# Index scores of a sparse-attention layer: every fourth weighted part summed by GpSimd instead of the vector engine

## What is computed

```python
logits = jnp.einsum('bqhd,bsd->bqhs', iqb, ik)
index = jnp.einsum('bqh,bqhs->bqs', iwb, jax.nn.relu(logits)) * idx_scale
index = jnp.where(causal[None], index.astype(jnp.float32), -jnp.inf)
_, sel = lax.top_k(index, topk)
```

## Time and profile before

| | |
|---|---|
| median of 3 runs | 3709.44 us (3705.83 to 3711.16) |
| profiled execution | 3711.52 us |
| its span, first to last instruction | 3709.0 us |
| mean granted TensorE clock | 0.968 of full speed |
| busy: PE, DVE, ACT, POOL | 3461.9, 2405.3, 1793.0, 1235.4 us |
| index units on VectorE, L1769 and L1772 | 38 and 266 |

### The profile page before, as it was taken

One profiled execution on the slowest core, in us unless ns is written; L12 is line 12 of the kernel. 1 busy time (PEld: TensorE's weight loads), 2 busy tenths in 40 slices (PEclk: granted clock), 3 DMA queues, 4 the chain that ended last, 5 costly groups with the idle time before them and its releaser, 6 DMA issues. The chain is left out here.

```text
span 3709.0 us, 55779 instructions
## 1 busy us (share of the span) xinstructions
PE 3461.9 (93%) x19082; PEld 2960.1 (80%) x19082; DVE 2405.3 (65%) x4983; ACT 1793.0 (48%) x3056; POOL 1235.4 (33%) x1944
## 2 busy tenths in 40 slices
PE   6999978899999999999999799699999999999998
PEld 6999867778888878788878688588888788888876
DVE  9999556667666766676774244765654657665354
ACT  3323235677776677767767333333333333333232
POOL 5454134454443432333222033433221425332021
PEclk9999899899999999999999899899999999999999
DMA  4344310000000000000000245332224452332444
GB/s 147 113 149 150 97 33 24 17 24 17 17 17 10 17 17 8 17 8 5 7 9 4 103 146 157 116 125 80 91 80 165 163 172 73 109 103 89 139 137 170
DMA packets 189699, 289.61 MB, mean 78 GB/s; under 512 B 33394, under 2 KB 129778, under 8 KB 189426
## 3 DMA queue, kind: packets, MB, share of 16 engines
q1 hardware_dynamic: 185300, 285.11, 23.4%
q10 hardware_dynamic: 4128, 1.05, 0.1%
HBM read 211.15 MB, written 74.97 MB: 77 GB/s over the span
## 5 line engine op out<-in xcount | busy, mean ns | idle before, releaser
L1669 ACT ACTIVATE shared<-a_ps_st 128x512 f32<-128x512 f32 x716 | 437.5, 615 | 288.4 <-PE a_ps_st L1555 147.7
L2712 PE MATMUL f_ps<-f_x_hi,f_w_hi 128*128 128x512 f32 x1232 | 482.5, 392 | 22.5 <-DVE f_w_lo L2849 22.5
L2712 PE MATMUL f_ps<-f_x_lo,f_w_hi 128*128 128x512 f32 x1232 | 481.6, 391 | 0.0
L2712 PE MATMUL f_ps<-f_x_hi,f_w_lo 128*128 128x512 f32 x1232 | 481.4, 391 | 0.0
L1579 PEld LDWEIGHTS a_ps_o<-a_vsl,shared 128*128 128x128 f32 x2176 | 294.5, 199 | 19.7 <-DVE a_fin L1886 0.7
L1377 POOL TENSOR_SCALAR a_tk<-a_tk,a_halves 128x1 f32<-128x1 f32 x336 | 106.1, 316 | 584.5 <-ACT a_junk_a L1676 582.7
L1579 PEld LDWEIGHTS a_ps_o<-a_dv,shared 128*128 128x128 f32 x2176 | 286.1, 194 | 12.5
L2712 PEld LDWEIGHTS f_ps<-f_x_hi,f_w_hi 128*128 128x128 f32 x1232 | 232.7, 189 | 73.0 <-DVE f_w_lo L2849 24.9
L1579 PE MATMUL a_ps_o<-a_vsl,shared 128*128 128x65 f32 x2176 | 286.1, 276 | 0.0
L1579 PE MATMUL a_ps_o<-a_dv,shared 128*128 128x65 f32 x2176 | 277.0, 271 | 0.0
L294 PE MATMUL p_ps<-pw_hi,px_hi 128*128 128x384 f32 (+1 forms) x672 | 228.1, 339 | 47.6 <-DVE pw_lo L399 30.4
(11 more groups left out here) (370 smaller groups left out, 8738.9 us busy)
## 6 DMA issues: line engine op xcount, KB each, us to landing
f_raw<-in_w_down SPq DMA_DIRECT2D x88, 512.0 KB, 3.5
px_raw<-in_x_t SPq DMA_DIRECT2D x48, 512.0 KB, 4.5
f_raw<-in_w_gate SPq DMA_DIRECT2D x44, 512.0 KB, 4.9
f_raw<-in_w_up SPq DMA_DIRECT2D x44, 512.0 KB, 4.8
g_scratch<-f_gs SPq DMA_DIRECT2D x22, 1024.0 KB, 7.6
f_raw<-g_scratch SPq DMA_DIRECT2D x88, 256.0 KB, 3.5
z_scratch<-p_z SPq DMA_DIRECT2D x16, 768.0 KB, 3.4
o_scratch<-a_oacc SPq DMA_DIRECT2D x32, 256.0 KB, 2.1
```

Source lines behind the costliest of these rows:

```text
L1669: act.activation(p_t[:, s % PT_RING, :], ps_st[s % ST_BANKS][:, :], ACT.Exp, scale=SCALE).then_inc(exp_done, 1)
L2712: mm = pe.matmul(out[:, :], w[:, j, k * P:(k + 1) * P], x[:, j, k], start=(k == 0 and i == 0), stop=(k == 3 and i == 2))
```

## The change

Of the index jobs, those whose number in `relu_no` leaves 3 when divided by 4 are summed by GpSimd, the others by VectorE as before. GpSimd has no single operation for it here: it multiplies the relu buffer by the weight in place (L1268), waits for its own semaphore, and adds the buffer to the index row (L1271). For h=0 it multiplies straight into the row (L1261). Instead of one semaphore that counts all sums there is one for each engine, and each wait looks up which engine's sum it means (`wait_sum`). GpSimd does the units of a step at the end of its own step s, after the threshold moves, the gathering and the splits of that step; VectorE still holds its units until the next step.

76 of the 304 jobs move: 32 of 512 columns, 16 of 384, 14 of 256 and 14 of 128. Where a tile has four chunks it is always the fourth chunk that GpSimd sums, for all eight heads.

```diff
--- before.py
+++ after.py
@@ -669,6 +669,7 @@
 NMAX_RING = 12
 PV_LAG = 3
 ONE_ROW = 94
+POOL_EVERY = 4
 SEL_COLS = 30
 SIDE_COST = {"max": 550, "cmax": 600, "idx": 680, "prep": 600, "aug": 150}
 CHORE_COST = {"peak": 0, "above": 300, "rank": 1150, "pick": 1250, "set": 900, "room": 0}
@@ -1064,6 +1065,12 @@
             reader.append(("evac", n_evac))
             if job[0] == "aug":
                 aug_no[job[1]] = turn_no[job]
+    sum_no, sums_by = {}, {"pool": 0, "dve": 0}
+    for job, r in relu_no.items():
+        who = "pool" if r % POOL_EVERY == POOL_EVERY - 1 else "dve"
+        sums_by[who] += 1
+        sum_no[job] = (who, sums_by[who])
+    nth_idx = list(relu_no)
     last_max = {job[1]: job for step in sides for job in step if job[0] == "max"}
     last_idx = {t: ("idx", t, IDX_HEADS - 1, plan.chunks[t] - 1) for t in range(2, TILES)}
     finish_at = {}
@@ -1177,7 +1184,7 @@
         exp_done = sem("a_exp_done")
         pv_done = sem("a_pv_done")
         relu_done = sem("a_relu_done")
-        index_done = sem("a_index_done")
+        index_done = {who: sem(f"a_index_{who}") for who in ("pool", "dve")}
         search_set = sem("a_search_set")
         counted = sem("a_counted")
         thr_moved = sem("a_thr_moved")
@@ -1227,6 +1234,41 @@
         def mask_d_value(t):
 
             return t + 1 if t < 2 else 2 + chunk_no[(t, plan.chunks[t] - 1)] + 1
+
+        def wait_sum(eng, job):
+
+            who, value = sum_no[job]
+            eng.wait_ge(index_done[who], value)
+
+        def wait_index(eng, t):
+
+            for c in range(plan.chunks[t]):
+                wait_sum(eng, ("idx", t, IDX_HEADS - 1, c))
+
+        def index_unit(eng, job):
+
+            _, t, h, c = job
+            who, _ = sum_no[job]
+            w = min(CHUNK, (t + 1) * P - c * CHUNK)
+            r = relu_no[job]
+            eng.wait_ge(relu_done, r + 1)
+            dst = index[t % 2][:, c * CHUNK:c * CHUNK + w]
+            weight = iw[:, t % 4, h:h + 1]
+            if h == 0:
+                eng.wait_ge(gate_in, 2 * (t + 1))
+                if t >= 4:
+                    eng.wait_ge(mask_d_done, mask_d_value(t - 2))
+                eng.tensor_scalar(dst, relu[:, r % RELU_RING, 0:w], weight, None, ALU.mult).then_inc(index_done[who], 1)
+            else:
+                wait_sum(eng, ("idx", t, h - 1, c))
+                part = relu[:, r % RELU_RING, 0:w]
+                if who == "dve":
+                    eng.scalar_tensor_tensor(dst, part, weight, dst, ALU.mult, ALU.add).then_inc(index_done[who], 1)
+                else:
+                    eng.tensor_scalar(part, part, weight, None, ALU.mult).then_inc(own, 1)
+                    begin.pool_owned[0] += 1
+                    eng.wait_ge(own, begin.pool_owned[0])
+                    eng.tensor_tensor(dst, dst, part, ALU.add).then_inc(index_done[who], 1)
 
         @block.sync
         def _(sp):
@@ -1344,7 +1386,7 @@
                 if t >= 4:
 
                     if t >= 6:
-                        pool.wait_ge(index_done, relu_no[last_idx[t - 4]] + 1)
+                        wait_index(pool, t - 4)
                     pool.wait_ge(fin_done, number[("S", t - 4, 1)] + 1)
                 at = KEY_COLS + IDX_DIM
                 pool.tensor_copy(iw[:, t % 4], zk[:, at:at + IDX_HEADS]).then_inc(gate_in, 1)
@@ -1441,6 +1483,9 @@
                         move_threshold(*c)
                     else:
                         waiting.append(c)
+                for job in sides[s]:
+                    if job[0] == "idx" and sum_no[job][0] == "pool":
+                        index_unit(pool, job)
 
         @block.tensor
         def _(pe):
@@ -1659,7 +1704,7 @@
                 act.wait_ge(side_done, scan_no[job] + 1)
                 if r >= RELU_RING:
 
-                    act.wait_ge(index_done, r - RELU_RING + 1)
+                    wait_sum(act, nth_idx[r - RELU_RING])
                 act.activation(relu[:, r % RELU_RING, 0:w], ps_side[side_no[job] % SIDE_BANKS][:, 0:w], ACT.Relu).then_inc(relu_done, 1)
 
             def exps(s):
@@ -1753,28 +1798,10 @@
                 settle()
                 dve.tensor_scalar(tile[:, 4 * g:4 * g + 4, col:col + 1], src, 1e20, None, ALU.min).then_inc(aug_set, 1)
 
-            def index_unit(job):
-                _, t, h, c = job
-                w = min(CHUNK, (t + 1) * P - c * CHUNK)
-                r = relu_no[job]
-                dve.wait_ge(relu_done, r + 1)
-                dst = index[t % 2][:, c * CHUNK:c * CHUNK + w]
-                weight = iw[:, t % 4, h:h + 1]
-                if h == 0 and c == 0:
-                    dve.wait_ge(gate_in, 2 * (t + 1))
-                if h == 0:
-                    if t >= 4 and c == 0:
-
-                        dve.wait_ge(mask_d_done, mask_d_value(t - 2))
-                    dve.tensor_scalar(dst, relu[:, r % RELU_RING, 0:w], weight, None, ALU.mult).then_inc(index_done, 1)
-                else:
-                    dve.wait_ge(index_done, relu_no[("idx", t, h - 1, c)] + 1)
-                    dve.scalar_tensor_tensor(dst, relu[:, r % RELU_RING, 0:w], weight, dst, ALU.mult, ALU.add).then_inc(index_done, 1)
-
             def peak(t, c):
 
                 if c == 0:
-                    dve.wait_ge(index_done, relu_no[last_idx[t]] + 1)
+                    wait_index(dve, t)
                 mine(dve.tensor_reduce(peaks[:, c:c + 1], index[t % 2][:, chunk_cols(t, c)], AX.X, ALU.max, apply_absolute_value=True))
 
             def set_search(t):
@@ -1899,16 +1926,16 @@
                 before = len(held)
                 for job in sides[s]:
                     if held and side_no[job] - side_no[held[0]] > SIDE_BANKS:
-                        index_unit(held.pop(0))
+                        index_unit(dve, held.pop(0))
                         before -= 1
                     if job[0] == "max":
                         mask(job)
                         if job == last_max[job[1]]:
                             set_aug(job[1])
-                    elif job[0] == "idx":
+                    elif job[0] == "idx" and sum_no[job][0] == "dve":
                         held.append(job)
                 while before > 0:
-                    index_unit(held.pop(0))
+                    index_unit(dve, held.pop(0))
                     before -= 1
                 for name, t, c in plan.chores[s]:
                     if name == "peak":
```

## The result

| | before | after |
|---|---|---|
| median of the runs (range) | 3710.3 us (3705.8 to 3711.6) | 3762.9 us (3762.3 to 3765.1) |
| ratio, with its 95% interval | | 1.0143 (1.0131 to 1.0156) |
| span of the profiled execution | 3709.0 | 3761.6 |

A forecast was written before the change was run, and what follows sets the result against it. TensorE was taken as the bound. New gaps of 9 + 3 us and 2 us of clock gave +14 on the profiled 3711.5 us, so 3725.5; less 2.1 for the median, 3723 us, range 3704 to 3746.

The forecast's parts named there:

- The bound, and VectorE's relief worth nothing: Attention phase: TensorE bounds; taking 41 us off VectorE gains about nothing on the path, at best 10 us.
- the 43 of the prediction: Attention phase: TensorE waits some 43 us for VectorE's row maxima, mostly between index-score stretches, and this should stay.
- the bursts: Stretches making index scores, one per query tile; GpSimd lateness should lengthen those of t=6 to 11 by 1 to 4 us.
- The prices: GpSimd at 512 columns: product 1.56 us, addition 1.27, a pair beside VectorE 3.8; 162 us more GpSimd work in all.
- GpSimd and VectorE in each other's way: In bursts, each pair costs VectorE 1.67 to 2.2 us; its 512-column units rise from 0.83 to about 1.2.
- Rival (4): Lock-bound: GpSimd operations and VectorE's index units exclude each other fully; 25 to 35 us lost, 3735 to 3746; chance 0.15.
- Who waits for the pair: Three parties wait: ScalarE's relus for buffers, VectorE's next-head unit, and the threshold move that ScalarE's next count needs.
- the budget: Bursts of t=6 to 11: GpSimd's busy time plus pairs, set against burst length, makes ScalarE 13.3 us late together.
- I take off 4 us: TensorE's lead over ScalarE spares it 0.7 us for each of six tiles, 4 us, which leaves 9.
- 9 + 3 us: New TensorE gaps: 9 us from the bursts of t=6 to 11, 3 from t=2 and 3, including late thresholds there.
- The clock: TensorE's granted clock: new gaps bring half-speed time; a third taken because the shown bursts run at 1.00; 2 us.
- The rule of the same paragraph: Attention phase: gaps bring about as much half-speed time, 122 us beside 112; for the new gaps 13 us, 6 lost.

The follow-up runs named there:

- t12: Changed kernel with GpSimd summing only for tiles t=12 to 15 (32 units), VectorE all the rest: 3713.7 us, 1.0015.
- dummy_nothr: dummy with ScalarE's counts also freed of waiting for threshold moves, so nobody waits for GpSimd's pairs: 3681.2 us.
- ground line: Kernel before, with ScalarE's counts comparing with a constant so they never wait for GpSimd's threshold moves: 3674.8 us.
- dummy: Changed kernel with all 304 sums on VectorE; GpSimd does same-width pairs on a spare tensor that nobody waits for: 3774.9 us, 1.0168.
- dummy_write: dummy with five memsets, which read nothing, in place of each GpSimd pair: 3740.9 us, 1.0083.
- The four kernels of the first section: Changed kernel with fifth relu buffer; GpSimd sums behind threshold move; no cross-engine sum waits below t=12; first two together: 3754.4, 3795.6, 3764.1, 3763.8 us.
- own_bufs: Changed kernel with a fifth relu buffer, two for GpSimd's jobs and three for VectorE's: 3754.4 us, 1.0116.
- nothr: Changed kernel with ScalarE's counts freed of waiting for threshold moves; relus and VectorE still wait for GpSimd: 3727.0 us.
- all_free: Changed kernel with freed counts, separate relu buffers per engine and, below t=12, no waits between the engines' sums: 3676.5 us.

## Why the prediction was wrong in size

- **The bound, and VectorE's relief worth nothing: right.** TensorE's waits for maxima did not fall: 40.2 us before and 39.7 after by the profile's rows (the 43 of the prediction holds VectorE's other results too). And t12 shows no gain from the relief. The loss lies in the bursts, 46.5 of 52 us.
- **The prices: right, if a little high.** GpSimd's product took 1.67 us (1.56 alone), the addition 1.38 (1.27 alone), a pair 3.05 us in the median (2.92 to 3.50) against the 3.8 forecast. By the best case of an elementwise loop over 512 elements in the Trainium skill (GPSIMD Engine Reference, section 3.1), 769 ns, the product would be half as long; the trace disagrees with 1672 ns.
- **GpSimd and VectorE in each other's way: over-sized.** VectorE's units rose to 0.91 us, not 1.2. Rival (4) would have put dummy_nothr 25 to 35 us above its ground line by its own sum; it stands 6 above. So (4), for all that it gave the nearest number, is not the mechanism. Nor do the two exclude each other fully: in the changed kernel 15 of VectorE's 512-column units began and ended within one product of GpSimd's (the one at 921.42 above is such), with 0.87 us in the median against 0.75 with GpSimd idle. The rule of a shared port pair held for the whole instruction (the Trainium skill, SBUF — State Buffer, Who interferes with whom) would not allow that; the trace disagrees with it. Contention can still matter by making GpSimd later; up to 32 us between dummy and dummy_write.
- **Who waits for the pair: one of three sized throughout, and the budget was of the wrong thing.** This is the step that failed. "9.67 + 3 x 3.8 = 21.1, 4.1 over the 17" adds busy time and compares it with the window, as if GpSimd worked without a pause. It works in order and waits for counts and quotients, so a pair is late wherever the round trip is longer than the ring allows, full or not: t=8 and 9 were to lose 0.7 and 1.3 us and lost 5.0 and 4.8, with GpSimd busy 72% of the burst of t=8. The relus' wait, 15.4 us, matches the forecast only in sum, and that is luck: it was to come most at t=6, 7, 10 and 11, and it is nothing at t=6, 0.3 us at t=7 and 4.1 at t=2. The thresholds, which I budgeted for t=2 and 3 only, took 21 us more on ScalarE, all of it in the bursts, and VectorE's 25.6 us were left at nothing but for t=2 and 3. "I take off 4 us" for TensorE's lead found nothing to stand on either: TensorE's waits for relus grew by 27.8 us. Instead of 9 + 3 us the gaps grew by 28.
- **The clock: sized 2 us, measured 25.** "The bursts run at 1.00 with gaps of their own, so I take a third" was the wrong choice of row: the seven rows ran at 1.00, but the burst of t=5, not among them, had 4.2 us of gaps and 0.87 already before. With the change the granted clock in the bursts of t=6 and 7 went to 0.87, part of them at 1.2 instead of 2.4 GHz, right where the gaps had opened. The rule of the same paragraph taken over the whole phase, as much half-speed time as gaps and half of it lost, gives about 15 us for 28 of gaps, and the trace has 25, so that rule was too small as well.

Why did each removed wait return so little? Because there is one lateness and three ways out of it. The four kernels of the first section left two of them, or all three. Shown: with none left (below t=12) it is 2 us, with only VectorE's 40, with only the threshold's 65 (on dummy's pairs), with relus and VectorE 52, with all three 53. The costs don't add. That the first waiter to meet the late engine takes the loss, and the others inherit it when that one is cured, is my reading of it: in own_bufs the counts' wait rose from 90.7 to 100.5 us when the relus' went, in nothr the relus' from 15.4 to 27.8 when the counts' went. Not tried: the relus' wait as the only one left, and the clock by itself, with gaps of the same length elsewhere.

## What to carry to other kernels

An engine that is busy 575 of 1530 us can be the wrong place for work, if others wait for it in order: ask not what it has free, but what stands behind the new work in its queue and how short the loop is in which it answers (here one step of ScalarE). When one late engine has several waiters, removing them one by one proves nothing; remove all of them, then give them back. And, in a kernel like this one, count each microsecond of a new gap on TensorE nearly twice (24.6 us of busy time came with 28.4 of gaps), until the granted clock of that stretch says otherwise; moving a wait (here GpSimd's for VectorE's quotients) behind the urgent work is the cheap edit to try first, worth 14 us in the kernel before.

## What the runs showed of the hardware that was not expected

- Three one-column operations on GpSimd, 0.19 + 0.29 + 0.19 us alone, took 0.64 + 0.81 + 0.65 us while VectorE ran 512-column units back to back. That is one case and a long one (their means over the phase are 0.23, 0.34 and 0.22), but in proportion it is far more than a product of 512 columns grew in dummy, from 1.58 alone to 1.92 in the mean. And the small operations are the urgent ones.
- VectorE and GpSimd slow each other without taking strict turns: a 0.75 us unit of VectorE's took 0.87 us in the median while it lay within a GpSimd product of some 1.6 us, and memsets, which only write, left it at its mean of before.
- A one-column operation is dear on ScalarE: 0.30 and 0.39 us, longer than the 0.19 and 0.29 on GpSimd.
- The granted clock falls with gaps, though not by their sum alone. Time in the phase, TensorE's busy time for the same matmuls, and gaps: all_free 1497, 1405.5, 91.6; before 1530, 1417.6, 112.4; nothr 1549, 1433.3, 115.5; after 1583, 1442.1, 140.9. 49 us of gaps between the first and the last come with 37 us of busy time; between before and nothr only 3 us of gaps come with 16.
